# Two blocks of a split product alternate between two accumulation banks, matmul by matmul

## What is computed

```python
# first block
proj = rms_norm(x, norm1_g) @ w_in          # 1024 -> 2304 + 1536 + 3072 columns
a = window_attention(...); b = hyena_branch(...); c = diff_attention(...)
x = x + (g0 * (a @ w_oa) + g1 * (b @ w_ob) + g2 * (c @ w_oc)) @ w_out
x = x + (silu(h2 @ ffn_w1) * (h2 @ ffn_w3)) @ ffn_w2      # d_ff 2816
# second block
proj = rmsnorm(x, attn_norm_g) @ w_in_2
o = concat(rmsnorm(fox_attention(...)), rmsnorm(stick_breaking_attention(...)))
x = x + o @ w_out_2
u = causal_dwconv(rmsnorm(x, ffn_norm_g) @ w_up)
x = x + (silu(gate) * val) @ w_down                        # d_ff 2816
return rmsnorm(x, final_norm_g)
```

## Time and profile before

| | us |
|---|---|
| median of 3 runs | 1744.34 |
| lowest, highest | 1743.65, 1744.95 |
| the profiled execution, its own time | 1748.23 |
| its span | 1746.4 |
| mean granted clock, as a share of full | 0.985 |
| TensorE busy with matmuls | 1677.4 |
| VectorE, ScalarE, GpSimd busy | 834.1, 659.9, 272.5 |

### The profile page before, as it was taken

One profiled execution on the slowest core, in us unless ns is written; L12 is line 12 of the kernel. 1 busy time (PEld: TensorE's weight loads), 2 busy tenths in 40 slices (PEclk: granted clock), 3 DMA queues, 4 the chain that ended last, 5 costly groups with the idle time before them and its releaser, 6 DMA issues.

```text
span 1746.4 us, 19135 instructions
## 1 busy us (share of the span) xinstructions
PE 1677.4 (96%) x7584; PEld 1316.7 (75%) x7584; DVE 834.1 (48%) x1330; ACT 659.9 (38%) x1150; POOL 272.5 (16%) x280
## 2 busy tenths in 40 slices
PE   5999999999999999999999998999999999999997
PEld 3557787777766787888888877776678788888886
DVE  5445455465356454333332224366654466666323
ACT  4332123454344433333332223455564344444221
POOL 3453305461012111000000002013210100000001
PEclk9999999999999999999999998999999999999999
DMA  6111112212121232332333322311101233233331
GB/s 225 61 61 48 49 53 86 71 49 61 60 62 48 99 107 73 97 97 97 96 97 96 97 84 65 102 60 36 37 25 61 73 97 97 97 97 97 109 97 72
DMA packets 39222, 139.51 MB, mean 80 GB/s; under 512 B 4332, under 2 KB 4972, under 8 KB 38941
## 3 DMA queue, kind: packets, MB, share of 16 engines
q1 hardware_dynamic: 39132, 138.29, 24.3%
HBM read 136.14 MB, written 2.10 MB: 79 GB/s over the span
## 4 chain that ended last, share of the span: by engine, by line
PE 87%; DVE 5%; POOL 3%; ACT 3%; issue 2%; DMA 0%; DVEq 0%; POOLq 0%; SPq 0%; ACTq 0%
PE ps L346 84%; PE ps L349 3%; ACT whi L1347 1%; POOL small L1801 1%; POOL small L1807 1%; DMA x<-in_x 0%; DVE wlo L778 0%; DVE W L1189 0%; POOL small L1804 0%; ACT junk L1359 0%; DVE st L1050 0%; DVE xs L789 0%; DVE sd L869 0%; DVE uT L922 0%; DVE uT L920 0%
## 5 line engine op out<-in xcount | busy, mean ns | idle before, releaser
L778 DVE TENSOR_TENSOR wlo<-wraw,whi 128x1024 fp32r<-128x1024 f32 (+2 forms) x220 | 267.1, 1215 | 523.9 <-ACT whi L1347 523.8
L346 PE MATMUL ps<-hThi,whi 128*128 128x512 f32 x1128 | 455.3, 404 | 2.2 <-DVE hTlo L794 1.3
L1347 ACT ACTIVATE whi<-wraw 128x1024 fp32r<-128x1024 f32 (+2 forms) x244 | 252.8, 1037 | 504.0 <-PE ps L346 498.5
L346 PE MATMUL ps<-hTlo,whi 128*128 128x512 f32 x1128 | 441.9, 392 | 0.0
L346 PE MATMUL ps<-hThi,wlo 128*128 128x512 f32 x1128 | 441.6, 392 | 0.0
L346 PEld LDWEIGHTS ps<-hThi,whi 128*128 128x128 f32 x1128 | 213.7, 189 | 58.1 <-issue 16.0
L346 PEld LDWEIGHTS ps<-hThi,wlo 128*128 128x128 f32 x1128 | 213.3, 189 | 45.7
L346 PEld LDWEIGHTS ps<-hTlo,whi 128*128 128x128 f32 x1128 | 213.7, 189 | 44.3 <-issue 2.9
L346 PE MATMUL ps<-whi,achi 128*128 128x512 f32 x352 | 136.9, 389 | 0.0
L346 PE MATMUL ps<-wlo,achi 128*128 128x512 f32 x352 | 136.9, 389 | 0.0
L346 PE MATMUL ps<-whi,aclo 128*128 128x512 f32 x352 | 136.9, 389 | 0.0
(11 more groups left out here) (270 smaller groups left out, 2199.1 us busy)
## 6 DMA issues: line engine op xcount, KB each, us to landing
wraw<-in_ws SPq DMA_DIRECT2D x236, 512.0 KB, 3.5
x<-in_x SPq DMA_DIRECT2D x4, 512.0 KB, 7.7
x<-in_x SPq DMA_DIRECT2D x1, 2048.0 KB, 8.2
out<-xs SPq DMA_DIRECT2D x8, 256.0 KB, 2.0
dec<-in_dec SPq DMA_DIRECT2D x1, 1024.0 KB, 15.2
wraw<-in_ws SPq DMA_DIRECT2D x4, 256.0 KB, 2.5
vec<-in_vec SPq DMA_DIRECT2D x1, 788.0 KB, 4.6
w<-in_w SPq DMA_DIRECT2D x1, 512.0 KB, 13.6
```

The lines of the kernel that those rows point to most:

```text
L346: return t.matmul(o, l, r, start=first, stop=last)
L778: v.tensor_tensor(wlo[h][:, 0:width(i)], wraw[h][:, 0:width(i)], whi[h][:, 0:width(i)].bitcast(F32), ALU.subtract).then_inc(lo_done[h], 1)
L1347: a.activation(whi[h][:, 0:width(i)], wraw[h][:, 0:width(i)], ACT.Copy).then_inc(hi_done[h], 1)
```

## The change

In groups with `rate` 1 and more than 128 columns, in every slot but the last, blocks 0 and 1 are issued together and then blocks 2 and 3: for each chunk and each of the three parts, one matmul into the even block's bank and then the same part into the odd block's bank. The number of matmuls, their operands and sizes, the order of the sums inside each bank and the last slot's order stay. On reaching the even block the code issues its `lo_done` and `take` waits and goes on to the odd block, which issues its own `take` and its `ready(k, b)` with the odd b, and then all twelve matmuls of the pair.

```diff
--- before.py
+++ after.py
@@ -357,23 +357,24 @@
                     w.wait_ge(lo_done[h], i // HL + 1)
                 if s == 0:
                     take(bank)
+                two = rate == 1 and n > 128 and not end
+                if two and b % 2 == 0:
+                    continue
                 for kk in range(2):
                     k = 2 * s + kk
                     ready(k, b)
                     ahi, alo = act(k)
-                    if mode == "tok":
-                        c0, c1 = kk * n, kk * n + n
-                        rows = slice(b * 128, b * 128 + 128)
-                        o = ps[bank][:, 0:n]
-                        mm(o, ahi[:, rows], whi[h][:, c0:c1], s == 0 and kk == 0, False)
-                        mm(o, ahi[:, rows], wlo[h][:, c0:c1], False, False)
-                        op = mm(o, alo[:, rows], whi[h][:, c0:c1], False, end and kk == 1)
-                    else:
-                        c0 = kk * n + b * 128
-                        o = ps[bank][:]
-                        mm(o, whi[h][:, c0:c0 + 128], ahi, s == 0 and kk == 0, False)
-                        mm(o, whi[h][:, c0:c0 + 128], alo, False, False)
-                        op = mm(o, wlo[h][:, c0:c0 + 128], ahi, False, end and kk == 1)
+                    for part in range(3):
+                        for b1 in (b - 1, b) if two else (b,):
+                            o = ps[BANK[name] + b1][:, 0:n] if mode == "tok" else ps[BANK[name] + b1][:]
+                            first_one, last_one = s == 0 and kk == 0 and part == 0, end and kk == 1 and part == 2
+                            if mode == "tok":
+                                rows, cols = slice(b1 * 128, b1 * 128 + 128), slice(kk * n, kk * n + n)
+                                stay, move = (ahi, ahi, alo)[part][:, rows], (whi, wlo, whi)[part][h][:, cols]
+                            else:
+                                c0 = kk * n + b1 * 128
+                                stay, move = (whi, whi, wlo)[part][h][:, c0:c0 + 128], (ahi, alo, ahi)[part]
+                            op = mm(o, stay, move, first_one, last_one)
                 if end:
                     op.then_inc(blocks, 1)
                     free[bank] = [freed(b)]
```

## The result

The changed kernel takes 1752.34 us (median of 10 runs, 1750.31 to 1755.58) against 1744.85 us before in the same sessions: ratio 1.0040, 95% interval 1.0029 to 1.0050. That is 7.5 us slower. The prediction had 1749.4, a range of 1744.8 to 1752.6, and "slower" at 0.57.

A forecast was written before the change was run, and what follows sets the result against it. TensorE's matmuls were taken as the only limit in the touched groups. Unchanged distance (0), four later starts (+3.52 us) and one clock drop (+1.6 us) gave +5.1 us on the median 1744.34: 1749.4 us, range 1744.8 to 1752.6.

The forecast's parts named there:

- The bank of the neighbour: All alternating matmuls: switching to the other bank at each start changes the distance between starts by 0.
- Rival C: Alternating matmuls: sharing a bank costs, alternation saves up to 0.0133 us each, 42 us, down to 1705; chance 0.08.
- The four waits: Later starts: +0.66 us at sq, +0.41 in sv, +1.09 in xo0 slot 0, +1.36 in xo0 slot 2; sum +3.52.
- The granted clock: Behind xo0 slot 2's longer pause: 3.2 us at half clock, +1.6 us, about 6 to 4 likely.
- I give it no sign: Other pauses between 1059 us and the end: the same 1.6 us can come or go, not counted in the sum.
- Rival D: Work behind sq and sv waits for other engines anyway, hiding 1.07 us: +2.45 us, 1746.8 us; chance 0.08.
- places 1 and 2: The later starts at sq (+0.66 us, waiting for bank 1) and in sv (+0.41 us, second pair waiting for bank 3).

The follow-up runs named there:

- e2: Kernel before plus alternation in every slot of the change except slot 0 and the xo groups, 2208 matmuls; 1746.77 us, ratio 1.0003.
- e9: The mended kernel plus the alternation in every group but xo0 and xo1, slot 0 included; 1738.72 us, ratio 0.9946.
- e10: The mended kernel plus the alternation outside xo0 and xo1, without slot 0 of each group; 1738.91 us, ratio 0.9952.
- the mended kernel: Kernel before, not alternating, with later memsets, other banks for sq and fl, another block order in xo0 slot 2; 1737.55 us, repeated 1739.27 us.
- e1: Kernel before with its matmul order kept, the even block asking early for the odd block's bank and input too; 1753.09 us, ratio 1.0042.
- e3: Kernel before plus alternation in xo0 and xo1 alone, 144 matmuls; 1748.81 us, ratio 1.0017.
- e4: Changed kernel plus nine more matmuls, into a bank nobody reads then, filling the pause of xo0 slot 2; 1750.18 us, ratio 1.0025.
- e5: Changed kernel without alternation in xo0 and xo1; 1749.79 us, ratio 1.0024 against the kernel before.
- e7: Changed kernel with e4's filling and four more matmuls filling the pause in front of sq; 1748.49 us, ratio 1.0011.

## Why the prediction was right, and where it was short

- **The bank of the neighbour: 0.** Right. The distance in `up` is unchanged, e2 gives 1.0003, and e9 and e10 lie 0.55 and 0.36 us under the mended kernel, less than the runs differ. Rival C needed 0.0022 us per matmul; e2's interval reaches down to -0.0006, or 1.0 us, and over 2208 matmuls that is 0.0005 us each at most. What section "A second HAM failure mode: psum-queue depth-cycling" of *TensorE: Matmul & The Clock Gate* (the Trainium skill) describes, a clock that oscillates when a kernel cycles through banks and TensorE idles briefly in between, didn't show either: the clock in `up` is 1.00 for 160 us, without a pause.
- **The four waits: +3.52 us.** Right in place and size: 0.65 of 0.66 at `sq`, 3.18 - 2.78 = 0.40 of 0.41 in `sv`, 4.02 - 2.85 = 1.17 of 1.09 in `xo0` slot 0. In slot 2 the pair starts 1340.82 - 1337.74 = 3.08 us behind the transposes (2.99 were forecast; the pause is 2.48 us, forecast 2.4), which makes 1.45 of 1.36. Together they are 3.67 us. e1 shows that these waits, with what they bring on, are the whole loss.
- **The granted clock: +1.6 us, too small.** This is the term of the sum that was mis-sized. What is left beside the waits is 7.5 - 3.7 = 3.8 us in the medians (3.3 by the ratio 1.0040). The one drop that the prediction counted, behind the pause of `xo0` slot 2, has the size that it gave, 1.56 us of 1.6, and came in two of the three profiled executions with that pause unfilled (the changed kernel and e1, not e3). The step that fell short is "I give it no sign": the prediction let the clock's drops elsewhere between `sq` and the end cancel. In the profiled executions of the changed kernel, e4, e5 and e7 the attention part took 1.9 us longer, at half clock, each time with the same sign. At `sq` the trace of the changed kernel lost another 1.6 us (its first and thirteenth matmul start 4.43 us apart, 2.85 before), but that isn't the longer pause: e2 has it with the pause of before, e5 has the longer pause without it.
- e7, where the two pauses are filled and less is lost, ties at least a part of this to them. A single drop comes or stays away behind the same pause, so this part can be given as an expectation only. The +5.1 us lie 2.4 us under the 7.5 measured, and the range holds the result by 0.3 us; that it does owes something to luck.
- **Rival D** (places 1 and 2 absorbed by attention behind them) fell: e5 alone is 4.2 us slower, and the pause in the attention part that could have taken the delay up is no shorter (1.69 us in the changed kernel, 1.68 before).
- What stays open: why the clock stays at half longer in the attention part when slot 0 of `sq`, `sk` and `sv` alternates, and how often; only one execution of each kernel was profiled. By its trace e7 should lose 3.7 + 1.9 us, and its median lost 1.9, so either the long stretch isn't in all its executions or they gain elsewhere. The intervals are 1 to 2 us each way, as wide as one drop of the clock.

## What to carry to other kernels

If a trace already has the event that an edit multiplies (here a bank switch once in six matmuls), its price stands there. Look instead at what an interleaving does to the conditions: two blocks issued together wait for the later one's bank and input, so cover is lost exactly where inputs arrive one by one, at the first slots of a group and behind a norm. Where one engine is the bound, count a lengthened pause for itself, and give the clock behind it, and in every later part with pauses, a range with a sign toward loss. A stretch at half clock behind a pause is charged to the edit only when the trace of before doesn't have it too. Spend the work on the pause: other banks and another block order and a later memset were worth 0.4% here, the alternation nothing.

## What the runs showed that was not expected

- GpSimd's memset of 2x4096 stretched VectorE's 128x1024 row scale from 0.75 to 4.08 us (it ends 0.56 us behind the memset), and not the weight subtraction beside it (1.22 us). The Trainium skill, *SBUF — State Buffer*, section "Who interferes with whom", says that GpSimd shares a port pair with VectorE, that a `tensor_scalar` can need that pair and then waits for the other's whole instruction, and that an operation with two inputs in SBUF contends with GpSimd's reads only. Both lines agree with it.
- The same pause of 2.48 us was followed by clock 0.50 in the changed kernel and by 1.00 in e3; around `sq` a pause of 1.30 us was followed by 0.50 (e2) and one of 1.96 us by 1.00 (e5). The kernel before, whose first three runs lay within 1.3 us, spread from 1743.4 to 1750.7 us over ten; at this size of effect a profile of one execution gives the waits exactly and the clock only as a draw.
